# Another order of the loads and of ScalarE between the routing stage and the last stage of a PEER encoder layer

## The chip, the cores and the metric

The kernel runs on one NeuronCore of a Trainium2 chip. The metric is the device time of one launch in microseconds (us). Five engines take part, each with its own instruction stream in a fixed order: TensorE (PE in the views, its weight loads PEld), VectorE (DVE), ScalarE (ACT), GpSimd (POOL) and SyncE (SP), which here does nothing but issue DMAs. An engine that waits for a semaphore lets nothing of its own stream pass.

## What is computed

Two layers of attention, pooling and a PEER block (product-key retrieval over 128 x 128 experts). The attention part is left out here; the change lies in the PEER block:

```python
def peer_ffn(xn, wq, sub_keys, expert_u, expert_v):
    xc = xn.reshape((B * S) // PEER_CHUNK, PEER_CHUNK, D)
    def one(x):
        q = (x @ wq).reshape(C, PEER_HEADS, 2, PEER_HALF)
        s = jnp.einsum('chpk,hpnk->chpn', q, sub_keys)
        top_s, top_i = lax.top_k(s, K)
        ...                                    # the 16 best of 16 x 16 sums: experts e, weights g
        u = jnp.take(expert_u, e, axis=0)
        h = jax.nn.gelu(jnp.einsum('cd,chkd->chk', x, u))
        v = jnp.take(expert_v, e, axis=0)
        return jnp.einsum('chk,chkd->cd', g * h, v)
```

There are 512 tokens, D is 1024, and 16384 experts have one U row and one V row of 1024 each.

## The kernel before, in words

For three of the four token tiles (384 tokens) the kernel does not gather: it multiplies all tokens with all experts and weighs the result with a routing matrix that is zero for experts that were not chosen. The experts are cut into 128 **U blocks** and 128 **V blocks** of 128 experts (512 KB each). The fourth tile goes by gathered rows (128 slots of 1 MB, an indirect DMA from GpSimd each); VectorE does a dot product (`dot`, L1474) and an addition (`add_row`, L1480) for every slot, all through the stages below.

A U block goes through four steps. SP loads it into one of two buffers `RAW` (`load_experts`, L308; it waits until the block two before it has been split). ScalarE rounds it to its high part `RH` (`hi`, L855). VectorE or GpSimd takes the low part `RL` (`low`). TensorE multiplies both with the tokens (24 matmuls), and ScalarE applies gelu. Blocks 0 to 75 (FILLED is 76) are done ahead, their gelu is stored in DRAM (`gelu_dram`); blocks 76 to 127 are done in the last stage, four in a turn of 8 V blocks (`hidden` on TensorE, `hidden_gelu` on ScalarE, L1061).

In the **routing stage** TensorE makes the routing matrix beside the U blocks; ScalarE puts it into two staging buffers, and SP stores each batch of 48 tokens in four pieces (`store_routing`, L347). Batch 7 is the last; it lies in the second staging buffer.

In the **last stage**, 16 turns of 8 V blocks, a V block q goes like this. SP loads it into one of two buffers `VRAW` (`position`, L387; it waits until the V block two before it has been split). VectorE weighs gelu with routing, `WF` (L1542), from `GB` or `GEL` (gelu) and `GC` (routing read back from DRAM). ScalarE rounds V and WF to `VHI` (L1071) and `WHI` (L1073), VectorE takes the low parts `VLO` (L1546) and `WLO` (L1549). TensorE takes two V blocks at a time (`output`, 36 matmuls). After pairs 0 and 1 it does two U blocks of the next turn, after pairs 2 and 3 the other two.

What lies between the two stages is written out by hand on each engine. On SP, in this order: piece 0 of batch 7, U block 78 (`load_next(2)`), pieces 1 to 3, `GB` of turn 0, U block 79, then a wait until all routing stores have landed (`routing_kept`, L419), `GC` half 0, V blocks 0 and 1, the gelu store of block 74, `GC` half 1, U block 80, the gelu store of block 75, U block 81, a wait until all gelu stores have landed, and `positions(0, ...)`. That last function, with `begun=True`, issues U blocks 82 and 83 at q = 1 (L401, L402), each behind the split of the block two before it, and only then V block 2. On ScalarE: `hi` of 78 and 79, gelu of 76, `hi` of 80, gelu of 77, `hi` of 81, then V block 0. TensorE does 76 to 79 in a row, but 78 needs the gelu of 76 to be taken, and 79 that of 77 (L770). The low parts of 76 and 77 are VectorE's, those of 78 to 81 GpSimd's; GpSimd goes on to the gathers of slots 21 and up behind the low part of 81.

Of the kernel before, what the change touches and what calls it, by code (L numbers as in the profile page):

```python
# [58 lines left out]
FILLED = 76  # L59
FIRST = 34  # L60
# [57 lines left out]
def program(nc, x, pos, inv_freq, ident, edge, vecs, gains, stream, peer_keys, peer_u, peer_v, peer_rows, out):  # L118
# [3 lines left out]
    with ctx:  # L122
# [161 lines left out]
        def _(sp):  # L284
# [6 lines left out]
            with sp.Fori(0, LAYERS) as l:  # L291
# [21 lines left out]
                def store_gelu(f, slot):  # L313
                    sp.wait_ge(S.gelu_done, count(l, "gelu_done", f + 1))
                    sp.dma_start(gelus[f], GS[:, slot, :]).then_inc(sems[f"gelu_stored{slot}"], 16)
# [31 lines left out]
                def store_routing(b, piece):  # L347


                    keys = slice(NK // 4 * piece, NK // 4 * (piece + 1))  # L350
                    if piece == 0:
                        sp.wait_ge(S.routing_taken, count(l, "routing_taken", 12 * b + 12))
                    sp.dma_start(route[b, :, keys], STAGE[b % 2][:, keys, :]).then_inc(sems[f"routing_stored{b % 2}"], 16)
# [33 lines left out]
                def position(it, q):  # L387
                    sp.wait_ge(S.v_low, count(l, "v_low", 8 * it + q - 1))
                    sp.dma_start(VRAW[:, q % 2, :], peer_v[l, 8 * it + q]).then_inc(sems[f"v_loaded{q % 2}"], 16)
# [20 lines left out]
                def load_next(n):  # L410
                    load_experts(J_U + FILLED + n, FILLED + n, n % 2)
# [4 lines left out]
                        apart(sp)  # L416
                    sp.dma_start(GB[:], gelus.rearrange("(g i) p t -> p g i t", i=QUAD)[:, 0]).then_inc(S.gelu_loaded, 16)

                def routing_kept():  # L419
                    for s in range(2):  # L420
                        sp.wait_ge(sems[f"routing_stored{s}"], count(l, f"routing_stored{s}", 256))
                        apart(sp)

                def load_routing_of_first():
                    sp.dma_start(GC[:, 0].rearrange("p b i t -> p b (i t)"),
                                 route.rearrange("b p (g i) t -> p g b (i t)", i=QUAD)[:, 0]).then_inc(S.routing_loaded0, 16)

                store_routing(7, 0)
                load_next(2)
                for piece in range(1, 4):  # L430
                    store_routing(7, piece)
                load_gelus_of_first()
                load_next(3)
                routing_kept()
                load_routing_of_first()
                position(0, 0)
                position(0, 1)
                store_gelu(FILLED - 2, 2)
                load_new(0)
                load_next(4)  # L440
                store_gelu(FILLED - 1, 3)
                load_next(5)
                for s in range(4):
                    sp.wait_ge(sems[f"gelu_stored{s}"], count(l, f"gelu_stored{s}", 4 * FILLED))
                    apart(sp)
# [374 lines left out]
        def _(act):  # L820
# [32 lines left out]
            with act.Fori(0, LAYERS) as l:  # L853
# [221 lines left out]
                def positions(n, it, j, now, next1, next2):  # L1075
                    at_q, k = AT_Q[n], first_slot(n)
                    for q in range(8):
                        position(it, q)
                        if q - 1 in at_q:
                            score_next(k + at_q.index(q - 1) + 1, j)  # L1080
                        if q == 3:
                            for m in (2, 3):
                                if now:
                                    hidden_gelu(it, m)
                                if next1:
                                    hi(it + 1, J_U + FILLED + m)
                    if 7 in at_q:
                        score_next(k + at_q.index(7) + 1, j)
                    if next1:
                        for m in (0, 1):  # L1090
                            hidden_gelu(it + 1, m)
                            if next2:
                                hi(it + 2, J_U + FILLED + m)

                def score_next(k, j):
                    if k < SLOTS:
                        score(k + THREE * j, k % RING)

                hi(0, J_U + FILLED + 2)
                hi(0, J_U + FILLED + 3)  # L1100
                for m in (0, 1):
                    hidden_gelu(0, m)
                    hi(1, J_U + FILLED + m)
                positions(0, 0, 0, True, True, True)
                with act.Fori(0, 3) as j:
                    for n in (1, 2, 3):
# [27 lines left out]
        def _(dve):  # L1134
# [55 lines left out]
            with dve.Fori(0, LAYERS) as l:  # L1190
# [329 lines left out]
                for k in range(S_ROUTE, S_ROUTE + S_TURN):  # L1520
# [1 line left out]
                    add_row(k, k % RING)  # L1522
                    dot((k + 1) % RING, (k + 1) // RING)
                    dve.drain()
                for n in range(J_U + FIRST + R_FILLS + 1 + S_TURN, J_U + FILLED + 2):
                    low(0, n)
                dve.drain()

# [55 lines left out]
        @block.gpsimd  # L1584
        def _(pool):
            for name, value in STARTS.items():
                pool.sem_inc(sems[name], value)
            pool.iota(IOTA[:], [[1, P]], base=0, channel_multiplier=0,
                      allow_small_or_imprecise_dtypes=True).then_inc(iota_made, 1)
            with pool.Fori(0, LAYERS) as l:  # L1590
                def low(i, k):

                    pool.wait_ge(S.high_part, count(l, "high_part", 4 * i + k + 1))
                    pool.tensor_tensor(RL[:, k % 4, :], RAW[:, k % 2, :], RH[:, k % 4, :].bitcast(F32),  # L1594
                                       ALU.subtract).then_inc(S.low_part, 1)

                with pool.Fori(0, J_GATE // 4) as i:
                    for k in range(4):
                        low(i, k)
                low(0, J_GATE)  # L1600
                low(0, J_GATE + 1)


                pool.wait_ge(S.latent_summed, count(l, "latent_summed", 1))
                apart(pool)
                pool.memset(GAB[:, 0:KD, :], 1.0)
                pool.drain()
                with pool.Fori(0, 4) as i:
                    for k in range(4):
                        low(i, J_GATE + k + 2)  # L1610
                        n = 4 * i + k
                        pool.wait_ge(S.taken_by_act, count(l, "taken_by_act", 8 + n + 1))
                        gab = GAB[:, bass.ds(n, 1), :].rearrange("p o t -> p (o t)")
                        apart(pool)
                        pool.tensor_scalar(GATE[:, k % 2, :], GATE[:, k % 2, :], 0.5, 0.5, ALU.mult, ALU.add)
                        pool.drain()
                        pool.tensor_tensor(gab, gab, GATE[:, k % 2, :], ALU.mult).then_inc(S.gate_applied, 1)
                low(0, J_WO + 2)
                low(0, J_WO + 3)
                with pool.Fori(J_WO // 4 + 1, (J_U + FIRST - 2) // 4) as i:  # L1620
                    for k in range(4):
                        low(i, k)

                def gather(k):

                    pool.wait_ge(S.slot_done, count(l, "slot_done", k - 2))
                    apart(pool)
                    pool.indirect_dma_start(ROWS[:, k % RING, :], None, peer_rows,  # L1628
                                            bass.IndirectOffsetOnAxis(ap=LIST[:, k:k + 1], axis=0)).then_inc(
                                                sems[f"rows_gathered{k % RING}"], 16)  # L1630

                def low_of(n):
                    low(0, n)

                for n in range(4 * ((J_U + FIRST - 2) // 4), J_U + FIRST):
                    low_of(n)
                low_of(J_U + FIRST)
                pool.wait_ge(S.experts_listed, count(l, "experts_listed", 1))
                for k in range(RING):
                    gather(k)  # L1640
                for i in range(8):
                    for k in range(2):
                        gather(2 * i + k + RING)
                for k in range(S_TURN):
                    gather(S_ROUTE + k + RING)
                pool.wait_ge(S.low_part, count(l, "low_part", J_U + FILLED + 2))
                apart(pool)
                for n in range(J_U + FILLED + 2, J_U + FILLED + 6):
                    low_of(n)
                for it in range(16):  # L1650
                    for q in range(8):
                        if q in AT_Q[it]:
                            k = first_slot(it) + AT_Q[it].index(q) + RING
                            if k < SLOTS:
                                gather(k)
                        if q == 3 and it + 1 < FULL:
                            low_of(J_U + FILLED + 4 * it + 6)
                            low_of(J_U + FILLED + 4 * it + 7)
                    if it + 2 < FULL:
                        low_of(J_U + FILLED + 4 * it + 8)  # L1660
                        low_of(J_U + FILLED + 4 * it + 9)
# [73 lines left out]
```

## Time and profile before

| | us |
|---|---|
| median of 3 runs | 3322.99 (3320.5 to 3329.58) |
| profiled execution, its own time | 3319.98 |
| its span in the profile | 3318.2 |
| PE busy | 3167.9 (95%) |
| DVE busy | 2493.8 (75%) |
| ACT busy | 1334.9 (40%) |
| POOL busy | 1101.8 (33%) |

All sums are made on the profiled execution. Times in the rows count from the start of its span, so layer 0's passage from routing to last stage lies at 865 to 950 us, layer 1's at 2520 to 2605 us. A row of a timeline begins with the start and the duration; in brackets is the idle time of the engine just before it and what ended it. A busy PE is not PE at its peak: ends of matmuls are modelled.

### The profile page before, as it was taken

What the parts mean: (1) busy time and instruction counts of PE and PEld (TensorE: products, weight loads), DVE (VectorE), ACT (ScalarE), POOL (GpSimd) and SP (SyncE); (2) the same over time, 40 slices, a digit from 0 to 9 for tenths busy, and PEclk for the clock granted to TensorE, in tenths of its full rate; (3) what the DMA queues carried; (4) which work ended last, traced back from release to release, by engine and by line L of the source; (5) the groups of instructions that cost most, each with busy time, mean ns of one, the idle gap of its engine ahead of it and who ended that gap; (6) DMA issues with size and microseconds to landing.
All of it is one profiled execution on the core that took longest, in us unless ns stands there. A gap on an engine that the chain in (4) does not pass through costs nothing.

```text
span 3318.2 us, 52436 instructions
## 1 busy us (share of the span) xinstructions
PE 3167.9 (95%) x16946; PEld 2787.0 (84%) x16946; DVE 2493.8 (75%) x4216; ACT 1334.9 (40%) x2351; POOL 1101.8 (33%) x625
## 2 busy tenths in 40 slices
PE   7999999999799999999999999999998999999999
PEld 5887799899788888887878877998997888888877
DVE  4555499899588888887645544998995888988876
ACT  4343333355344334343444333333553343443434
POOL 3443354300134333341044433453001333334310
PEclk9999999999999999999999999999998999999999
DMA  3211244589899998988622112445898889999895
GB/s 110 83 51 51 102 132 132 184 303 326 316 348 328 335 331 325 336 323 328 222 96 70 51 57 102 133 134 183 312 324 321 330 319 344 343 336 348 328 333 200
DMA packets 249512, 774.05 MB, mean 233 GB/s; under 512 B 20352, under 2 KB 124928, under 8 KB 216320
## 3 DMA queue, kind: packets, MB, share of 16 engines
q1 hardware_dynamic: 212480, 503.53, 43.2%
q0 software_dynamic: 36864, 268.45, 21.4%
q8 instruction: 84, 1.38, 0.2%
q14 instruction: 84, 0.69, 0.1%
HBM read 689.59 MB, written 82.31 MB: 233 GB/s over the span
## 4 chain that ended last, share of the span: by engine, by line
PE 53%; DVE 13%; issue 11%; DMA 10%; DVEq 7%; ACT 4%; POOL 1%; SPq 0%; ACTq 0%; POOLq 0%
PE PS L468 16%; PE PS L470 15%; PE PS L469 15%; DMA VRAW<-in_peer_v 7%; DVEq L1560 6%; DVE ROWS L1474 4%; DVE VLO L1546 4%; PE PS L754 3%; DVE X L1480 2%; ACT VHI L1071 2%; PE PS L648 2%; DMA ROWS<-in_peer_rows,LIST 2%; DVE WLO L1549 1%; PE PS L710 1%; PE PS L642 1%
## 5 line engine op out<-in xcount | busy, mean ns | idle before, releaser
L468 PE MATMUL PS<-XH,RH 128*128 128x384 f32 (+1 forms) x2720 | 980.7, 361 | 38.4 <-ACT GEL L1063 25.7
L1594 POOL TENSOR_TENSOR RL<-RAW,RH 128x1024 fp32r<-128x1024 f32 x298 | 742.6, 2501 | 749.9 <-ACT RH L861 749.4
L469 PE MATMUL PS<-XL,RH 128*128 128x384 f32 (+1 forms) x2720 | 954.4, 351 | 0.0
L470 PE MATMUL PS<-XH,RL 128*128 128x384 f32 (+1 forms) x2720 | 954.4, 351 | 0.0
L1628 POOL DMA_INDIRECT ROWS<-in_peer_rows,LIST x256 | 291.1, 1137 | 1301.5 <-DVE X L1480 1260.4
L468 PE MATMUL PS<-VHI,WHI 128*128 128x512 f32 x1536 | 606.2, 395 | 45.9 <-DVE WLO L1549 45.8
L469 PE MATMUL PS<-VLO,WHI 128*128 128x512 f32 x1536 | 602.8, 392 | 0.0
L470 PE MATMUL PS<-VHI,WLO 128*128 128x512 f32 x1536 | 602.7, 392 | 0.0
L468 PEld LDWEIGHTS PS<-XH,RH 128*128 128x128 f32 x2720 | 515.1, 189 | 67.6 <-issue 27.0
L469 PEld LDWEIGHTS PS<-XL,RH 128*128 128x128 f32 x2720 | 515.6, 190 | 27.0
L470 PEld LDWEIGHTS PS<-XH,RL 128*128 128x128 f32 x2720 | 513.7, 189 | 28.7
L1546 DVE TENSOR_TENSOR VLO<-VRAW,VHI 128x1024 fp32r<-128x1024 f32 x256 | 317.0, 1238 | 198.5 <-ACT VHI L1071 198.3
L861 ACT ACTIVATE RH<-RAW 128x1024 fp32r<-128x1024 f32 x384 | 404.1, 1053 | 105.8 <-DMA RAW<-in_peer_u 46.8
L468 PEld LDWEIGHTS PS<-VHI,WHI 128*128 128x128 f32 x1536 | 291.5, 190 | 116.5 <-DVE VLO L1546 47.1
L1071 ACT ACTIVATE VHI<-VRAW 128x1024 fp32r<-128x1024 f32 x256 | 270.5, 1057 | 290.7 <-DMA VRAW<-in_peer_v 207.3
L470 PEld LDWEIGHTS PS<-VHI,WLO 128*128 128x128 f32 x1536 | 291.0, 189 | 61.4
L469 PEld LDWEIGHTS PS<-VLO,WHI 128*128 128x128 f32 x1536 | 291.6, 190 | 58.3
L1073 ACT ACTIVATE WHI<-WF 128x384 fp32r<-128x384 f32 x256 | 133.5, 522 | 511.7 <-DVE WF L1542 511.6
L1480 DVE SCALAR_TENSOR_TENSOR X<-ROWS,SHARE,X 128x1024 f32<-128x1024 f32 x256 | 326.8, 1277 | 7.4 <-ACT SHARE L1031 7.4
L1474 DVE SCALAR_TENSOR_TENSOR ROWS<-ROWS,XG 128x1024 f32<-128x1024 f32 x256 | 311.5, 1217 | 9.4 <-DMA ROWS<-in_peer_rows,LIST 9.4
L1542 DVE TENSOR_TENSOR WF<-GEL,GC 128x384 f32<-128x384 f32 x128 | 194.3, 1518 | 37.9 <-issue 37.9
L1549 DVE TENSOR_TENSOR WLO<-WF,WHI 128x384 fp32r<-128x384 f32 x256 | 189.1, 739 | 0.0
(235 smaller groups left out, 3318.5 us busy)
## 6 DMA issues: line engine op xcount, KB each, us to landing
RAW<-in_peer_u SPq DMA_DIRECT2D x256, 512.0 KB, 4.5
VRAW<-in_peer_v SPq DMA_DIRECT2D x256, 512.0 KB, 5.7
RAW<-in_stream SPq DMA_DIRECT2D x128, 512.0 KB, 3.5
route_dram<-STAGE SPq DMA_DIRECT2D x64, 768.0 KB, 6.9
GC<-route_dram SPq DMA_DIRECT2D x64, 768.0 KB, 10.4
gelu_dram<-GS SPq DMA_DIRECT2D x152, 192.0 KB, 4.6
GB<-gelu_dram SPq DMA_DIRECT2D x32, 768.0 KB, 12.6
GEL<-gelu_dram SPq DMA_DIRECT2D x6, 768.0 KB, 7.5
```

What stands on the lines that cost most here:

```text
L468: pe.matmul(acc, sh, mh, start=first, stop=False)
L469: pe.matmul(acc, sh, ml, start=False, stop=False)
L470: return pe.matmul(acc, sl, mh, start=False, stop=last)
L861: act.activation(RH[:, j % 4, :], RAW[:, j % 2, :], ACT.Copy).then_inc(S.high_part, 1)
L1071: act.activation(VHI[:, q % 4, :], VRAW[:, q % 2, :], ACT.Copy).then_inc(S.v_high, 1)
L1474: dve.scalar_tensor_tensor(ROWS[:, c, 0:D], ROWS[:, c, 0:D], 1.0, XG[:], ALU.mult, ALU.mult, accum_out=DOT[:, c:c + 1]).then_inc(S.dotted, 1)
L1480: dve.scalar_tensor_tensor(X[:, DT, :], ROWS[:, c, D:], SHARE[:, c:c + 1], X[:, DT, :], ALU.mult, ALU.add).then_inc(S.slot_done, 1)
L1546: dve.tensor_tensor(VLO[:, q % 4, :], VRAW[:, q % 2, :], VHI[:, q % 4, :].bitcast(F32), ALU.subtract).then_inc(S.v_low, 1)
L1549: dve.tensor_tensor(WLO[:, q % 4, :], WF[:, q % 2, :], WHI[:, q % 4, :].bitcast(F32), ALU.subtract).then_inc(S.weighted_low, 1)
L1560: dve.drain()
L1594: pool.tensor_tensor(RL[:, k % 4, :], RAW[:, k % 2, :], RH[:, k % 4, :].bitcast(F32), ALU.subtract).then_inc(S.low_part, 1)
L1628: pool.indirect_dma_start(ROWS[:, k % RING, :], None, peer_rows, bass.IndirectOffsetOnAxis(ap=LIST[:, k:k + 1], axis=0)).then_inc(sems[f"r ...
```

## The change

On SP, U block 79 is issued between pieces 1 and 2 of batch 7; `routing_kept` takes the buffers that it waits for, and only the first staging buffer is waited for ahead of V blocks 0 and 1 and U block 80. The wait for the second one, `GC` half 0 and half 1 and U block 81 stand behind them. On ScalarE, `hi` of 78 and gelu of 76, `hi` of 79 and gelu of 77 alternate, V blocks 0 and 1 come next, and `hi` of 80 and 81 stand behind V block 1. The low parts of 78 and 79 go from GpSimd to VectorE.

```diff
-                def routing_kept():
-                    for s in range(2):
+                def routing_kept(slots):
+                    for s in slots:
                         sp.wait_ge(sems[f"routing_stored{s}"], count(l, f"routing_stored{s}", 256))
                         apart(sp)
...
                 store_routing(7, 0)
                 load_next(2)
-                for piece in range(1, 4):
-                    store_routing(7, piece)
+                store_routing(7, 1)
+                load_next(3)
+                store_routing(7, 2)
+                store_routing(7, 3)
                 load_gelus_of_first()
-                load_next(3)
-                routing_kept()
-                load_routing_of_first()
+                routing_kept((0,))
                 position(0, 0)
                 position(0, 1)
+                load_next(4)
                 store_gelu(FILLED - 2, 2)
+                routing_kept((1,))
+                load_routing_of_first()
                 load_new(0)
-                load_next(4)
+                load_next(5)
                 store_gelu(FILLED - 1, 3)
-                load_next(5)
...
                         position(it, q)
                         if q - 1 in at_q:
                             score_next(k + at_q.index(q - 1) + 1, j)
+                        if q == 1 and n == 0:
+                            for m in (0, 1):
+                                hi(1, J_U + FILLED + m)
...
-                hi(0, J_U + FILLED + 2)
-                hi(0, J_U + FILLED + 3)
                 for m in (0, 1):
+                    hi(0, J_U + FILLED + 2 + m)
                     hidden_gelu(0, m)
-                    hi(1, J_U + FILLED + m)
...
-                for n in range(J_U + FIRST + R_FILLS + 1 + S_TURN, J_U + FILLED + 2):
+                for n in range(J_U + FIRST + R_FILLS + 1 + S_TURN, J_U + FILLED + 4):
                     low(0, n)
...
-                pool.wait_ge(S.low_part, count(l, "low_part", J_U + FILLED + 2))
+                pool.wait_ge(S.low_part, count(l, "low_part", J_U + FILLED + 4))
                 apart(pool)
-                for n in range(J_U + FILLED + 2, J_U + FILLED + 6):
+                for n in range(J_U + FILLED + 4, J_U + FILLED + 6):
                     low_of(n)
```

SP behind U block 79 of the kernel before; GC is the routing read back, VRAW a V block, RAW a U block, gelu_dram a gelu store:

```order
L421 ISA
L425 DMA GC<-route_dram 128x8x192 [waits routing_stored0,routing_stored1]
L388 REGISTER_ALU
L389 DMA VRAW<-in_peer_v 128x1024 [waits v_low]
L388 REGISTER_ALU
L389 DMA VRAW<-in_peer_v 128x1024 [waits v_low]
L314 REGISTER_ALU
L315 DMA gelu_dram<-GS 128x384 [waits gelu_done]
L375 REGISTER_ALU
L376 DMA GC<-route_dram 128x8x192 [waits weighted]
```

SP at the same place of the changed kernel, from the load of GB on:

```order
L421 ISA
L388 REGISTER_ALU [waits routing_stored0]
L389 DMA VRAW<-in_peer_v 128x1024 [waits v_low]
L388 REGISTER_ALU
L389 DMA VRAW<-in_peer_v 128x1024 [waits v_low]
L310 REGISTER_ALU
L294 ISA [waits low_part]
L294 DMA RAW<-in_peer_u 128x1024
L314 REGISTER_ALU
L315 DMA gelu_dram<-GS 128x384 [waits gelu_done]
L425 DMA GC<-route_dram 128x8x192 [waits routing_stored1]
```

The first GC load, which led this row of issues, now stands behind two V blocks, U block 80 and a gelu store, and the wait for the second staging buffer has moved with it.

ScalarE of the kernel before, from `hi` of 78 to the first V block (RH is a U block's high part, GEL a gelu, VHI and WHI the high parts of V and WF):

```order
L861 ACTIVATE RH<-RAW 128x1024 [waits block_used,block_loaded0]
L861 ACTIVATE RH<-RAW 128x1024 [waits block_used,block_loaded1]
L1062 REGISTER_ALU
L1063 ACTIVATE GEL<-PS 128x384 [waits block_used]
L858 REGISTER_ALU
L861 ACTIVATE RH<-RAW 128x1024 [waits block_used,block_loaded0]
L1062 REGISTER_ALU
L1063 ACTIVATE GEL<-PS 128x384 [waits block_used]
L861 ACTIVATE RH<-RAW 128x1024 [waits block_used,block_loaded1]
L1068 ISA
L1071 ACTIVATE VHI<-VRAW 128x1024 [waits pair_done,v_loaded0]
L1073 ACTIVATE WHI<-WF 128x384 [waits weighted]
```

ScalarE of the changed kernel, from the first V block to `hi` of 80 and 81 (lines have moved by two; ACTED and SHARE belong to a gathered slot):

```order
L1073 ACTIVATE VHI<-VRAW 128x1024 [waits pair_done,v_loaded0]
L1075 ACTIVATE WHI<-WF 128x384 [waits weighted]
L1073 ACTIVATE VHI<-VRAW 128x1024 [waits pair_done,v_loaded1]
L1075 ACTIVATE WHI<-WF 128x384 [waits weighted]
L1030 REGISTER_ALU
L1031 ACTIVATE ACTED<-DOT 128x1 [waits dotted]
L1033 ACTIVATE SHARE<-ACTED,GATES 128x1 [waits acted]
L860 REGISTER_ALU
L863 ACTIVATE RH<-RAW 128x1024 [waits block_used,block_loaded0]
L863 ACTIVATE RH<-RAW 128x1024 [waits block_used,block_loaded1]
```

The two high parts of 80 and 81 stood ahead of V block 0 and now stand behind WHI of V block 1.

## Rows read from the trace of the kernel before

**Rows 1.** Busy time by stretch: engines' busy us and count, granted clock, DMA share, GB/s
```profile
870.00:880.00 10.00, 10.00 (x60) 10.00 (x59) 3.66 (x4) 3.30 (x7) 2.76 (x2) 1.00 1.01 396
...
910.00:920.00 10.00, 7.44 (x27) 6.07 (x28) 9.52 (x15) 3.95 (x8) 2.97 (x3) 0.83 0.80 273
```

**Rows 2.** Timeline of PE, layer 0, from U block 78 to the fourth output pair
```profile
890.17 0.68 PE L468 MATMUL PS<-XH,RH 128*128 128x384 f32 x1 [8.29 <-ACT GEL L1063]
...
902.01 0.68 PE L468 MATMUL PS<-XH,RH 128*128 128x384 f32 x1 [5.21 <-ACT GEL L1063]
...
912.56 0.79 PE L468 MATMUL PS<-VHI,WHI 128*128 128x512 f32 x1 [4.67 <-DVE WLO L1549]
...
915.59 0.40 PE L469 MATMUL PS<-VLO,WHI 128*128 128x512 f32 x1
915.82 0.39 PE L470 MATMUL PS<-VHI,WLO 128*128 128x512 f32 x1
...
947.41 0.49 PE L468 MATMUL PS<-VHI,WHI 128*128 128x512 f32 x1 [0.42 <-DVE WLO L1549]
```

**Rows 3.** Waits of PE in layer 1 from 2520 us on: total, times, longest
```profile
PE PS L468 <- ACT GEL L1063: 12.2, 2, 8.8
```

**Rows 4.** Timeline of ACT, layer 0
```profile
888.61 1.06 ACT L861 ACTIVATE RH<-RAW 128x1024 fp32r<-128x1024 f32 x1 [10.31 <-DMA RAW<-in_peer_u]
...
902.16 1.06 ACT L861 ACTIVATE RH<-RAW 128x1024 fp32r<-128x1024 f32 x1 [0.28 <-DMA RAW<-in_peer_u]
903.13 1.04 ACT L1071 ACTIVATE VHI<-VRAW 128x1024 fp32r<-128x1024 f32 x1
...
910.93 0.52 ACT L1073 ACTIVATE WHI<-WF 128x384 fp32r<-128x384 f32 x1 [5.41 <-DVE WF L1542]
...
911.58 0.29 ACT L1031 ACTIVATE SHARE<-ACTED,GATES 128x1 f32<-128x1 f32 x1
912.21 1.06 ACT L1071 ACTIVATE VHI<-VRAW 128x1024 fp32r<-128x1024 f32 x1 [0.33 <-DMA VRAW<-in_peer_v]
```

**Rows 5.** Timeline of SP (issues of DMAs), layer 0
```profile
874.38 0.36 SPq L294 DMA_DIRECT2D RAW<-in_peer_u  x1
885.37 0.38 SPq L425 DMA_DIRECT2D GC<-route_dram  x1
885.97 1.25 SPq L389 DMA_DIRECT2D VRAW<-in_peer_v  x2
...
893.46 13.33 SPq L294 DMA_DIRECT2D RAW<-in_peer_u  x3
907.40 0.33 SPq L389 DMA_DIRECT2D VRAW<-in_peer_v  x1
```

**Rows 6.** Timeline of DVE, layer 0
```profile
892.66 0.56 DVE L1542 TENSOR_TENSOR WF<-GB,GC 128x384 f32<-128x384 f32 x1 [18.46 <-DMA GC<-route_dram]
...
910.34 0.56 DVE L1542 TENSOR_TENSOR WF<-GB,GC 128x384 f32<-128x384 f32 x1 [0.16 <-issue]
...
915.00 0.56 DVE L1542 TENSOR_TENSOR WF<-GB,GC 128x384 f32<-128x384 f32 x1 [0.16 <-issue]
915.48 1.22 DVE L1546 TENSOR_TENSOR VLO<-VRAW,VHI 128x1024 fp32r<-128x1024 f32 x1
...
921.28 0.55 DVE L1549 TENSOR_TENSOR WLO<-WF,WHI 128x384 fp32r<-128x384 f32 x1
...
924.41 5.75 DVE L1542 TENSOR_TENSOR WF<-GEL,GC 128x384 f32<-128x384 f32 x1 [0.24 <-issue]
```

**Rows 7.** Timeline of POOL, layer 0: pairs of low parts
```profile
901.58 4.71 POOL L1594 TENSOR_TENSOR RL<-RAW,RH 128x1024 fp32r<-128x1024 f32 x2 [9.49 <-ACT RH L861]
...
951.59 5.75 POOL L1594 TENSOR_TENSOR RL<-RAW,RH 128x1024 fp32r<-128x1024 f32 x2 [1.16 <-ACT RH L861]
```

**Rows 8.** DMA issue of V block 0 (885.97): KB, us from issue to landing
```profile
VRAW<-in_peer_v SPq DMA_DIRECT2D x1, 512.0 KB, 7.9
```

**Rows 9.** DMA issue of V block 2 (907.40), the same columns
```profile
VRAW<-in_peer_v SPq DMA_DIRECT2D x1, 512.0 KB, 4.8
```

## The prediction

> **What bounds the kernel now.** I read the page's busy line first (TensorE is 95% busy, so a gain must come from its gaps), then TensorE's timeline for its gaps at the place of the change, then the timelines of the engine that ends each gap, and last the landings of the DMAs behind them.
>
> In layer 0 TensorE stops three times between U block 77 and the first output pair: 8.29 us ahead of block 78, 5.21 ahead of 79, 4.67 ahead of the pair [rows 2]. In layer 1 the first two are 12.2 us together [rows 3]. The first two wait for ScalarE's gelu, and the reader is to see why that is late: it stands behind `hi` of block 79, whose load was issued at 874.38 [rows 5] and reached ScalarE at 888.61, after 14.2 us [rows 4]. The DMA engines are full there (share 1.01 at 870 to 880 [rows 1]). The third gap waits for VectorE, and that wait is the one that counts: the last stage cannot start before V blocks 0 and 1 and their WF are split. VectorE made WF of block 0 at 892.66, as soon as the routing had landed, but WF of block 1 only at 910.34 [rows 6], since ScalarE's in-order stream stood at `hi` of 80 and 81 until 903.13 [rows 4]. From there VectorE paces: 4.66 us for each V block (910.34 to 915.00), and WLO of block 3 ends at 921.83 (921.28 and 0.55) [rows 6]. TensorE's first pair runs from 912.56 to about 922.2: 7 matmuls take 3.03 us, the other 29 take 0.23 each, 6.6 [rows 2]. So at pair 1 VectorE and TensorE arrive within half a us of each other, and at pair 3 TensorE waits 0.42 [rows 2]. I measure the change at WLO of block 3 and at pair 3.
>
> **TensorE's own gaps: worth nothing by themselves.** U block 79 cannot be issued earlier: its load waits for the split of 77, which let it go at 874.38 before, and does now. It lands earlier only because two routing pieces and GB no longer stand ahead of it. Then blocks 78 and 79 follow 77 without a gap, and TensorE is done with them long before VectorE has the first pair ready. It then waits for WLO of block 1. The cover of this edit is that wait; if 79 landed late as before, nothing would change either. VectorE splits 78 and 79 in a stretch in which it stood still for 18.46 us [rows 6], so that move is free too.
>
> **The first half, a gain.** V blocks 0 and 1 no longer stand behind 80 and 81 on ScalarE, so WF of block 0 decides, and that waits for the first GC load. GC could not be issued before the last routing store landed (issued at 885.37 [rows 5]), and it now stands in SP's queue behind V blocks 0 and 1, U block 80 and a gelu store. V block 0, issued right behind GC, landed at 885.97 + 7.9 = 893.9 [rows 5, 8], 1.3 us after GC: that is what 512 KB costs in the full queue. The routing stores themselves end 1.3 us later (79 ahead of two of them); that is no added cost, as GC stood behind 79 before as well. Three blocks at 1.3 and 192 KB at 0.5 make 4.4 us: WF of block 0 at 892.66 + 4.4 = 897.1. Bounds: 0, if the queue delays GC not at all, and 5.7, if the later routing stores count in full. One V block takes 4.66, so WF of block 1 starts at 901.8 and ends at 902.3, against 910.9: **8.6 us earlier**.
>
> **The second half, the gain given back.** V block 2 stands on SP behind U blocks 82 and 83, whose loads wait for the splits of 80 and 81. Before, these were made while V block 0 was still waiting: GpSimd's pair of them ran at 901.58 for 4.71 [rows 7], SP got past at 906.79 (893.46 and 13.33), and V block 2 went out at 907.40 [rows 5]. Now `hi` of 80 and 81 come after WHI of block 1, so the chain runs from the end of WF of block 1 (call it 0):
> - WHI of 1 and the slot's SHARE: 910.93 to 911.87 in [rows 4], so 0.9 to 1.0.
> - `hi` of 80: 1.06 [rows 4], done at 2.0. `hi` of 81 follows beside GpSimd.
> - GpSimd's two low parts: 4.71 with VectorE out of the way, 5.75 with VectorE at work [rows 7]. VectorE is at work on slots here, so I take 5.75: 7.8.
> - SP issues 83, then V block 2: 906.29 to 906.79 before for the one, as much again for the other, so 1.0: 8.8.
> - V block 2 lands: 4.8 [rows 9]. It has the same two U blocks ahead of it as before, so I take this, 13.6; the row of the full queue, 7.9 [rows 8], is the other end.
> - VHI 1.06 [rows 4], VLO of 2 at 14.7. From there to the end of WLO of 3 it was 915.48 to 921.83, 6.35 [rows 6]: 21.05.
>
> Before, the same way took 921.83 - 910.90 = 10.93. The loss is **10.1 us**. Net at WLO of block 3: 10.1 - 8.6 = +1.5.
>
> **TensorE's clock.** Pair 0 now starts 8.6 earlier, at about 904, and takes 9.6 as before, and TensorE then stands still for over 9 us until WLO of block 3 at 923.4. After the stop of 4.67 us its first 7 matmuls went at 0.43 us instead of 0.23, and the granted clock of 910 to 920 was 0.83 [rows 1, 2], a mean of the two levels 1.2 and 2.4 GHz. I charge the same again for pair 1: 7 x 0.2 = 1.4. Pair 1 starts 1.2 later than before (923.4 against 922.2); with 1.4 more and 0.42 of slack at pair 3 [rows 2] that is 2.2 for TensorE, 1.5 for VectorE. I take 2 in each layer.
>
> **Sum.** The profiled execution took 3319.98 us (span 3318.2, and 1.8 around it). Two layers at +2 give 3324. The median of the three runs is 3.0 above that execution, so the forecast on its scale is **3327**. About 0.3% (10 us) is what a measurement of this kernel tells from no change; this is inside.
>
> **A rule of the Trainium skill against the change.** GpSimd's pair took 4.71 us in one place and 5.75 in the other, and a WF that takes 0.56 elsewhere took 5.75 at 924.41 [rows 6, 7]: the two engines hinder each other. The Trainium skill, SBUF — State Buffer, "Who interferes with whom", says that a VectorE operation with two SBUF inputs and a GpSimd operation take an exclusive pair of ports, each for its whole instruction, whichever starts first. By it both slot instructions could go ahead of a low part; as an estimate with VLO's 1.22 for each, the pair ends 4.71 + 2.4 long, 1.4 later than I took, and the forecast would be 3330. The trace shows one such turn (5.75 is 1.04 over 4.71), not two.
>
> **Rival 1, GC is not delayed** (DMAs overlap, and the small reads of GC slip between the blocks). WF of block 0 stays at 892.66, 4.4 earlier than taken, and GpSimd's pair takes 4.71: net at WLO of 3 is 1.5 - 4.4 - 1.0 = -3.9, with TensorE's cold start about -2.5 to -4 in a layer. 3315 to 3318 on the scale of the runs. For it: landings are pipelined. Against it: V block 0 landed after GC, in the order of issue [rows 8]. Chance 0.14.
>
> **Rival 2, the gain stays** because V block 2 is free as soon as VLO of block 0 is done, as before. Then the whole last stage starts 8.6 us earlier in both layers: 3306. It decides by whether SP reaches V block 2 before the split of 81; the code puts 82 and 83 ahead. Chance 0.06.
>
> **Rival 3, slower: V block 2 lands late.** The gathers of slots 21 and 22 stand on GpSimd behind the low part of 81, and with VectorE early their slots are free, so both go out in one go exactly when V blocks 2 and 3 do, behind 82 and 83. If V block 2 takes the 7.9 us of a full queue [rows 8] instead of 4.8, that is 3.1 more; a second turn of VectorE ahead of GpSimd adds about 1.2, and a layer costs 2 + 3.1 + 1.2 = 6.3, the kernel +13: 3336. It becomes slower by over 0.3% from about 3 us more than my sum in a layer, that is a landing of 7.8. For it: a busy queue costs that much 20 us earlier. Against it: the queue has run dry by then. Chance 0.18.
>
> The Trainium skill, DMA: Bandwidth & Descriptors, "Queues, rings and completion order", adds that a DMA engine goes round the queues packet by packet, so SP's V blocks and GpSimd's gathers would share; an estimate by it doubles V block 2's 1.3, +1.3 in a layer, which no row here shows apart.
>
> **How the numbers follow.** Forecast as summed 0.62, rivals 0.14, 0.06, 0.18. Forecast and rival 1 are within 0.3%: 0.76; faster 0.06; slower 0.18. The forecast's own bounds are about 3323 to 3331; with rival 1 below and the near part of rival 3 above the range is 3315 to 3335.
>
> **What would show it.** In the changed trace: TensorE without the waits for GEL (right for the first edit), WF of block 0 at 896 to 898, GpSimd's pair of low parts behind WHI of block 1, V block 2 issued 8 to 9 us after WF of block 1, a new stop of TensorE of 8 to 10 us between pair 0 and pair 1, and `WLO` of block 3 at 922 to 925. It is wrong if WF of block 0 stays below 894, if V block 2 is issued before the low part of 81, or if V block 2's landing takes over 8 us.

## The result, and the profile after

The change makes the kernel slightly slower: **3332.02 us**, the median of 12 runs (3321.41 to 3338.95), against 3316.74 for 12 runs of the kernel before beside it (3305.94 to 3329.58). The ratio is **1.0042, with a 95% interval of 1.0029 to 1.0056**. The profiled execution took 3326.28 us, with a span of 3324.5. The forecast was 3327 and the range 3315 to 3335, so the time lies inside; but the loss of 0.42% is over the 0.3% that I had named as what a measurement can tell, and I had given a loss of that size only 18%.

In the passage from routing to the last stage nearly everything went as summed. TensorE's timeline in layer 0, from U block 78 to the second output pair (start, duration, in brackets the idle time ahead and what ended it), answers to [rows 2]:

```profile
901.61 0.79 PE L470 MATMUL PS<-VHI,WHI 128*128 128x512 f32 x1 [12.52 <-DVE WLO L1552]
...
920.90 0.79 PE L470 MATMUL PS<-VHI,WHI 128*128 128x512 f32 x1 [8.18 <-DVE WLO L1552]
921.49 0.63 PE L471 MATMUL PS<-VLO,WHI 128*128 128x512 f32 x1
921.91 0.63 PE L472 MATMUL PS<-VHI,WLO 128*128 128x512 f32 x1
```

The three stops have become two. No wait for GEL is left, in neither layer; both stops wait for VectorE's WLO. The timeline of VectorE (DVE) over the same stretch answers to [rows 6]:

```profile
894.74 0.56 DVE L1545 TENSOR_TENSOR WF<-GB,GC 128x384 f32<-128x384 f32 x1 [10.21 <-DMA GC<-route_dram]
...
899.39 0.56 DVE L1545 TENSOR_TENSOR WF<-GB,GC 128x384 f32<-128x384 f32 x1 [0.16 <-issue]
...
902.67 3.39 DVE L1477 SCALAR_TENSOR_TENSOR ROWS<-ROWS,XG 128x1024 f32<-128x1024 f32 x1
906.00 0.08 DVE L1477 DVE_READ_ACCUMULATOR ROWS<-ROWS,XG 128x1 f32 x1
906.23 2.49 DVE L1545 TENSOR_TENSOR WF<-GB,GC 128x384 f32<-128x384 f32 x1 [0.16 <-issue]
914.42 1.23 DVE L1549 TENSOR_TENSOR VLO<-VRAW,VHI 128x1024 fp32r<-128x1024 f32 x1 [5.69 <-ACT VHI L1073]
...
920.22 0.55 DVE L1552 TENSOR_TENSOR WLO<-WF,WHI 128x384 fp32r<-128x384 f32 x1
```

WF of V blocks 0 and 1 now come 4.65 us apart (before 17.68 [rows 6]), and the time gained is lost again behind WF of block 2: VLO of block 2 waits 5.69 us for VHI. The reason stands on SP (issues of DMAs) and on GpSimd (POOL), which answer to [rows 5, 7]; the last row is V block 2's landing (KB, us from issue to landing), as in [rows 9]:

```profile
873.24 0.35 SPq L294 DMA_DIRECT2D RAW<-in_peer_u  x1
...
885.94 0.40 SPq L425 DMA_DIRECT2D GC<-route_dram  x1
...
905.15 3.66 SPq L294 DMA_DIRECT2D RAW<-in_peer_u  x2
909.00 11.80 SPq L389 DMA_DIRECT2D VRAW<-in_peer_v  x4
```

```profile
901.96 6.34 POOL L1597 TENSOR_TENSOR RL<-RAW,RH 128x1024 fp32r<-128x1024 f32 x2 [29.48 <-ACT RH L863]
```

```profile
VRAW<-in_peer_v SPq DMA_DIRECT2D x1, 512.0 KB, 4.3
```

GpSimd begins the low parts of 80 and 81 only at 901.96, SP gets past U blocks 82 and 83 behind them, and V block 2 goes out at 909.00.

**Where the loss is.** I compared the starts of WLO, one for each V block, between the two traces. Between the last WLO of turn 0 and the last WLO of turn 11 the kernel before takes 564.35 us in layer 0 and 558.05 in layer 1, the changed one 571.49 and 564.86: 7.1 and 6.8 more, in a stretch in which the change alters no instruction. One trace of each kernel cannot price the loss: in the seven traces of the experiments below this stretch of a layer takes 550.5 to 571.3 us, and the kernel before lies among them. But the two traces show what is new. VectorE's waits in layer 0, 960 to 1560 us (total, times, longest), in the kernel before:

```profile
DVE VLO L1546 <- ACT VHI L1071: 59.9, 22, 3.7
DVE WF L1542 <- issue: 27.3, 96, 0.8
```

and in the changed kernel:

```profile
DVE VLO L1549 <- ACT VHI L1073: 53.6, 18, 5.8
DVE WF L1545 <- issue: 45.8, 94, 7.8
```

"issue" is idle time in which the engine waits for nothing that the profile shows. It was 0.8 us at most ahead of a WF, and is now 7.8, with 18.5 us more in all. The long ones stand at the start of turns 4, 7 and 10 in both layers. VectorE's timeline at turn 4 of layer 0, before:

```profile
1101.17 0.08 DVE L1474 DVE_READ_ACCUMULATOR ROWS<-ROWS,XG 128x1 f32 x1
1102.05 0.56 DVE L1542 TENSOR_TENSOR WF<-GB,GC 128x384 f32<-128x384 f32 x1 [0.79 <-issue]
1105.55 1.27 DVE L1546 TENSOR_TENSOR VLO<-VRAW,VHI 128x1024 fp32r<-128x1024 f32 x1 [2.95 <-ACT VHI L1071]
1106.74 2.75 DVE L1549 TENSOR_TENSOR WLO<-WF,WHI 128x384 fp32r<-128x384 f32 x1
...
1111.99 0.56 DVE L1542 TENSOR_TENSOR WF<-GB,GC 128x384 f32<-128x384 f32 x1 [0.16 <-issue]
```

and after:

```profile
1105.88 0.08 DVE L1477 DVE_READ_ACCUMULATOR ROWS<-ROWS,XG 128x1 f32 x1
1112.95 0.56 DVE L1545 TENSOR_TENSOR WF<-GB,GC 128x384 f32<-128x384 f32 x1 [6.99 <-issue]
1113.42 1.22 DVE L1549 TENSOR_TENSOR VLO<-VRAW,VHI 128x1024 fp32r<-128x1024 f32 x1
1114.56 0.55 DVE L1552 TENSOR_TENSOR WLO<-WF,WHI 128x384 fp32r<-128x384 f32 x1
...
1117.61 0.56 DVE L1545 TENSOR_TENSOR WF<-GB,GC 128x384 f32<-128x384 f32 x1 [0.16 <-issue]
```

Turns 1 to 12 are a hardware loop on VectorE (`dve.Fori(0, 4)`, three turns to a pass), so turns 4, 7 and 10 are the places where it returns to its start. A stop of 7 us costs much less than 7: from the last row of the old turn to WF of the second block it is 10.74 us before (1101.25 to 1111.99) and 11.65 after (1105.96 to 1117.61), since before VectorE waited there for VHI, 2.95, and its WLO took 2.75 instead of 0.55. The lateness of the WLO starts against the kernel before grows, from the last V block ahead of a return to the second one behind it, by 0.96, 1.81, 1.53, 1.64, 0.82 and 0.79 us at the six returns, 7.6 together. That is 7.6 of the 13.9 us above; the rest lies between the returns, where the two executions drift apart and together by some us. The page's lists of DMA queues (packets, MB, share) say where to look: the kernel before has

```profile
q14 instruction: 84, 0.69, 0.1%
```

and the changed one

```profile
q14 instruction: 115, 0.93, 0.1%
```

These are 31 packets of instructions more. At each of the six returns the trace has four of them, 8 KB each, inside the stop or just behind it (at 1110, 1110, 1115 and 1119 us for turn 4); most of the others come once in each pass.

What the change has to do with that loop is a count. It moves the low parts of U blocks 78 and 79 from GpSimd to VectorE, two instructions each (a register operation and the subtraction) in VectorE's program *ahead* of the loop. The loop stands 4 instructions later than before.

### The profile page after: what moved, and what is told of

The parts are those of the page before. It is cut to its first block, busy times and chain, and to the rows that moved or that the text cites. A ratio compares the mean times of both kernels' runs of the same rounds, so it can differ in the third digit from the quotient of the medians.

```text
span 3324.5 us, 52436 instructions
## 1 busy us (share of the span) xinstructions
PE 3158.4 (95%) x16946; PEld 2775.1 (83%) x16946; DVE 2490.4 (75%) x4220; ACT 1336.3 (40%) x2351; POOL 1088.8 (33%) x621
## 4 chain that ended last, share of the span: by engine, by line
PE 53%; DVE 13%; issue 12%; DMA 10%; DVEq 7%; ACT 3%; POOL 1%; ACTq 0%; SPq 0%; POOLq 0%
PE PS L470 16%; PE PS L472 15%; PE PS L471 15%; DMA VRAW<-in_peer_v 7%; DVEq L1563 6%; DVE VLO L1549 4%; DVE ROWS L1477 4%; PE PS L756 3%; DVE X L1483 2%; PE PS L650 2%; ACT VHI L1073 1%; DVE WLO L1552 1%; DMA ROWS<-in_peer_rows,LIST 1%; POOL RL L1597 1%; PE PS L712 1%
## 5 line engine op out<-in xcount | busy, mean ns | idle before, releaser
L1597 POOL TENSOR_TENSOR RL<-RAW,RH 128x1024 fp32r<-128x1024 f32 x294 | 730.4, 2494 | 758.4 <-ACT RH L863 757.9
L992 ACT ACTIVATE GS<-PS 128x384 f32<-128x384 f32 x152 | 74.8, 492 | 273.8 <-PE PS L472 273.6
```

## The experiments

Theory A, formed from this: the stops come from where the loop stands in the program. The rivals were that the stops belong to what the change does in the passage (VectorE splitting 78 and 79, its order against GpSimd), and that the passage itself costs the whole loss, with the stops harmless.

**e1: the kernel before, with nothing changed but the loop's place.** Four memsets of one column each, on VectorE, ahead of the `dve.drain()` that stands before the last stage:

```
+                for i in range(4):
+                    dve.memset(HGB[:, i:i + 1], 0.0)
                 dve.drain()
```

> The kernel before, with four extra one-element writes on VectorE (64 ns kind, into a tile that is dead there) between the last low part and V block 0, where VectorE stands still for 18 us. Nothing else moves; every later VectorE instruction lies four further in its program, as in the changed kernel. Theory A (the loss comes from the place of VectorE's loop over the turns in its program: at each return the loop has to be loaded again): the stops of about 7 us at the start of turns 4, 7 and 10 appear here too, and the kernel gets 8 to 15 us slower than before, ratio 1.0025 to 1.0045. Theory B (the loss comes from the passage: TensorE's new stop and cold start, and the phase in which the last stage begins): no change, ratio 0.999 to 1.001.

Measured: ratio 1.0023 (1.0008 to 1.0038). The waits of VectorE, 960 to 1560 us:

```profile
DVE WF L1544 <- issue: 47.8, 96, 8.1
```

There are stops of 6.8 to 8.1 us at turns 4, 7 and 10 of both layers, and 114 instruction packets. Nothing else of the change is in this kernel, so the stops come from the place, and they cost it about 0.23%, 7.6 us: 1.3 us for each return, as in the steps above. The ratio is just under the 1.0025 that theory A had as its lower end.

**e2: the change, with the two low parts back on GpSimd**, so that the loop stands where it stood before:

```
-                for n in range(J_U + FIRST + R_FILLS + 1 + S_TURN, J_U + FILLED + 4):
+                for n in range(J_U + FIRST + R_FILLS + 1 + S_TURN, J_U + FILLED + 2):
...
-                pool.wait_ge(S.low_part, count(l, "low_part", J_U + FILLED + 4))
+                pool.wait_ge(S.low_part, count(l, "low_part", J_U + FILLED + 2))
...
-                for n in range(J_U + FILLED + 4, J_U + FILLED + 6):
+                for n in range(J_U + FILLED + 2, J_U + FILLED + 6):
```

> The changed kernel with one part undone: the low parts of U blocks 78 and 79 stay on GpSimd, so VectorE's program is that of before, instruction for instruction, while SP and ScalarE have the new order. Theory A: the stops at turns 4, 7 and 10 are gone, and the time is that of before within 4 us, ratio 0.999 to 1.001. Theory B: as slow as the changed kernel, ratio about 1.004.

Measured: ratio 1.0001 (0.9983 to 1.0019). VectorE's waits in the same stretch:

```profile
DVE WF L1545 <- issue: 27.4, 97, 0.8
```

Without the four instructions no return stops, with the rest of the change in place. VectorE's wait ahead of WF of block 0 is 21.7 us (10.2 in the changed kernel, 18.46 before), and no loss of time can be measured.

**e3 and e5: the change, with the loop moved further on.** VectorE keeps the low parts; 124 memsets (e3) or 16 (e5) put the loop 128 or 20 instructions later than in the kernel before. They run while VectorE waits for GC.

```
+                for i in range(124):
+                    dve.memset(NUMBER[:, i:i + 1], 0.0)
                 dve.drain()
```

> The changed kernel with 124 extra one-element writes on VectorE at the same place (about 7 us in a stretch where it waits for 10), so that its loop over the turns lies 128 instructions behind its place in the kernel before. Theory A, if programs are loaded in pieces of 128 instructions (the 8 KB of the instruction queue's packets at 64 bytes each): the stops are gone again, ratio 0.999 to 1.002. If the pieces are larger: stops remain, ratio about 1.004. Theory B: ratio about 1.004.

> The change plus 16 memsets of one column on VectorE, so that its loop over the last stage stands 20 instructions later than in the kernel before (the change alone: 4 later, with stops of 6 to 7 us at the loop's return; 128 later: none). Theory A, three blocks: instructions come in blocks and the engine holds two; the loop of 271 instructions spans three blocks only if it begins within about 15 instructions of a place that recurs every 256. The kernel before does not stop and 4 later does, so 20 later is past the narrow zone: no stops ahead of WF (wait for issue back to 0.8 us on average), instruction packets back to about 84, ratio 1.0000 to 1.002 to the kernel before. Theory B, a broad zone (any place from 4 later up to some 100): stops of 7 us as in the change, ratio 1.003 to 1.005. Theory C, the stops have nothing to do with the loss: no stops, yet a ratio of 1.004.

Measured: e3 1.0020 (1.0005 to 1.0036), e5 1.0020 (1.0000 to 1.0040). The waits of VectorE in e3, then in e5, and e5's instruction packets:

```profile
DVE WF L1547 <- issue: 28.0, 99, 0.8
```

```profile
DVE WF L1547 <- issue: 26.7, 98, 0.8
```

```profile
q14 instruction: 84, 0.69, 0.1%
```

The stops are gone in both, so the place that stops is narrow: 4 instructions on it stops, 20 on and 128 on it does not. That is theory A as e5's text puts it, and the broad zone falls. The size of the pieces stays open: e3's text had the stops gone only with pieces of 128 instructions, but a narrow zone that recurs every 256 fits these four places as well. Both ratios are under the changed kernel's 1.0042, though both kernels do *more* on VectorE. Theory C, no stops and yet 1.004, is at the very end of e5's interval; e1, where the stops alone cost time, speaks against it.

**e6: the changed kernel itself again**, on the chip and beside the kernels of e5 and e7.

> The changed kernel itself, on the same chip as the two beside it, so that its ratio to the kernel before can be set against theirs. Theory A: 1.003 to 1.005, stops at turns 4, 7 and 10 of both layers, and the kernel with 16 memsets more is 0.2 to 0.4% faster than this one though it does more. If the loss was the chip's of the first measurement: about 1.000 here.

Measured: 1.0054 (1.0033 to 1.0074), with 114 instruction packets and stops of 7.3 to 8.6 us at the six returns:

```profile
DVE WF L1545 <- issue: 46.9, 94, 8.6
```

The loss is not the first chip's. Against e5's 1.0020 the stops are worth 1.0054 / 1.0020 = 1.0034, somewhat more than e1's 1.0023. The intervals of all three are wide, so I put the stops at 0.2 to 0.35%.

The table gathers the closing branch of the loop, read from the branch instructions in VectorE's trace: the time from the branch to the next instruction, a register operation that waits for nothing.

| kernel | loop later by | three returns of layer 0, us | of layer 1, us | q14 packets | ratio |
|---|---|---|---|---|---|
| before | 0 | 0.32, 0.27, 0.27 | 0.28, 0.26, 0.26 | 84 | 1 |
| changed | 4 | 6.17, 7.00, 6.73 | 6.83, 6.02, 5.99 | 115 | 1.0042 |
| e1 | 4 | 7.04, 7.32, 6.64 | 6.60, 6.95, 6.01 | 114 | 1.0023 |
| e6 | 4 | 6.51, 7.78, 6.93 | 7.22, 6.89, 7.04 | 114 | 1.0054 |
| e2 | 0 | 0.32, 0.27, 0.27 | 0.28, 0.26, 0.26 | 84 | 1.0001 |
| e5 | 20 | 0.35, 0.32, 0.31 | 0.32, 0.29, 0.29 | 84 | 1.0020 |
| e3 | 128 | 0.33, 0.30, 0.29 | 0.33, 0.30, 0.29 | 86 | 1.0020 |

In the kernels whose return stops, the lateness of WLO grows there as in the changed one: by 0.8 to 2.1 us in e1, 9.4 together, and by 1.3 to 2.6 in e6, 11.2 together. In e2 to e5 and e7 it grows by 0.02 at most. Such a step spans a few us of each execution, so the drift between executions hardly touches it. TensorE's weight loads, ScalarE and GpSimd return to their loops in the last stage within 0.06 to 0.26 us in every kernel, so of these engines VectorE's loop alone stops.

One pass of the loop is 273 instruction records from one closing branch to the next. The same engine's outermost loop, over the two layers, is a jump back over the whole program: it stops in every kernel, 5.30 us in the one before and 3.96 to 5.51 in the others. So a jump back that stops takes VectorE some 4 to 8 us, and one that does not 0.3.

The Trainium skill, Runtime: NRT & Kernel Launch, "Instruction fetch mechanics", has the rule for this: an engine takes in its instructions in blocks of 16 KiB, 256 instructions, holds two of them, and a taken branch to a place outside the two has to wait for a load. The traces agree: by that rule, as an estimate, a loop of 273 lies in two blocks at most places and in three at about 16 of 256, which fits a stop at 4 and none at 0, 20 or 128. The page gives no price for such a wait; here it is 6.0 to 7.8 us. That the place decides is shown by the runs; that the blocks are the reason is the page's account, which no run here shows by itself.

**e4: V block 2 first.** The second half of my sum says that V block 2 is late because it stands behind U blocks 82 and 83 on SP. From e2, one line (q is the V block after whose issue SP goes on to the next U blocks, `begun` is turn 0):

```
-                        if q == 1:
+                        if q == (3 if begun else 1):
```

> As the second kernel (low parts of 78 and 79 on GpSimd, VectorE's program that of before), and on SP, in turn 0, V blocks 2 and 3 ahead of U blocks 82 and 83. It prices the wait that gives back the gain: V block 2 then goes out as soon as VLO of block 0 is done. If that wait is what eats the gain (my sum: 10 us in a layer), VectorE reaches WLO of block 3 some 8 us earlier than before, TensorE's second stop is about 0 to 1 us, and the kernel is 12 to 17 us faster than before, ratio 0.995 to 0.9965. If the gain is eaten elsewhere, ratio 0.999 to 1.001.

Measured: 0.9989 (0.9971 to 1.0007), far less than the 0.995 to 0.9965 of the main expectation: most of the gain is lost elsewhere. WLO of block 3 starts 45.75 us after the low part of U block 77 in layer 0 and 48.11 in layer 1, against 48.49 and 49.30 in e2. V block 2 is no longer late; the timeline of VectorE shows what is late next:

```profile
903.50 2.49 DVE L1545 TENSOR_TENSOR WF<-GB,GC 128x384 f32<-128x384 f32 x1 [0.16 <-issue]
...
912.58 1.23 DVE L1477 SCALAR_TENSOR_TENSOR ROWS<-ROWS,XG 128x1024 f32<-128x1024 f32 x1 [3.78 <-DMA ROWS<-in_peer_rows,LIST]
```

A gathered row (ROWS) holds VectorE's dot product for 3.78 us, and with it WF of block 3. GpSimd had issued its gather only behind the two low parts (e4's GpSimd):

```profile
899.21 6.37 POOL L1597 TENSOR_TENSOR RL<-RAW,RH 128x1024 fp32r<-128x1024 f32 x2 [16.71 <-ACT RH L863]
905.73 1.09 POOL L1631 DMA_INDIRECT ROWS<-in_peer_rows,LIST  x1 [0.15 <-issue]
```

**e7: the row first as well.** e4, with GpSimd's first gather of the last stage ahead of the low parts of 80 and 81:

```
-                for n in range(J_U + FILLED + 2, J_U + FILLED + 6):
+                for n in range(J_U + FILLED + 2, J_U + FILLED + 4):
                     low_of(n)
...
                                 gather(k)
+                        if it == 0 and q == 0:
+                            for n in range(J_U + FILLED + 4, J_U + FILLED + 6):
+                                low_of(n)
```

> The change with the low parts of U blocks 78 and 79 back on GpSimd, with V blocks 2 and 3 loaded ahead of U blocks 82 and 83 in turn 0, and now also with GpSimd's gather of the first row of the last stage ahead of its split of U blocks 80 and 81. In the version without this last step the dot product ahead of WF of V block 3 waited 3.8 us for that row, which stood 6.4 us behind the split. Theory: V block 3 comes 3 to 4 us earlier in each layer, and the whole ends at 0.996 to 0.998 of the kernel before. Rival: the next wait (the V blocks of turn 0's second half, or the split that now ends 1 us later) takes it back, and the ratio stays at 0.998 to 1.000, as without the step (0.9989).

Measured: 0.9997 (0.9980 to 1.0015), as the rival said. In its trace the step does what it should: WLO of block 3 comes 43.22 and 43.03 us after the low part of 77, where the kernel before has 48.31 and 47.37, and TensorE's second stop is down to

```profile
915.54 0.49 PE L470 MATMUL PS<-VHI,WHI 128*128 128x512 f32 x1 [2.40 <-DVE WLO L1552]
```

That is 4.3 to 5.1 us a layer, 9.4 or 0.28% in all, and the interval ends at 0.20%. So by this one trace a part of it is lost again further on. The second pair of turn 1 on TensorE still starts 5.1 us earlier after the low part of 77 than in the kernel before, in both layers, so it is lost later than that; where was not followed to the end of the stage. A next wait is to be seen in the trace, 1.78 us for the next gathered row at 918.39. Neither e4 nor e7 can be told from the kernel before.

## Why the prediction was right, and where it was wrong

**TensorE's gaps are worth nothing by themselves: right.** The waits for GEL are gone in both layers, the time is not: TensorE waits 12.52 and 8.18 us for WLO instead.

**The first half: right, with the delay of GC somewhat too large.** Counted from the issue of U block 79 (874.38 before [rows 5], 873.24 after), WF of block 0 moved from +18.28 to +21.50, 3.2 us later; I had taken 4.4. The end of WF of block 1 moved from +36.52 to +26.71, 9.8 earlier against 8.6. Rival 1, no delay of GC at all, falls. WF of block 0 itself is at 894.74 and WLO of block 3 at 920.22, each a little ahead of the signs that I had given (896 to 898, 922 to 925), mostly since U block 79 was issued 1.1 us earlier in this execution.

**The second half: right nearly to the step.** From the end of WF of block 1 (899.95) V block 2 goes out after 9.05 us (said 8.8), it lands in 4.3 (said 4.8), VLO of block 2 starts at 14.47 (said 14.7) and WLO of block 3 ends at 20.82 (said 21.05). Errors inside it cancel: GpSimd's pair of low parts took 6.34, not 5.75, while SP then had V block 2 out after 0.7 us instead of 1.0 and the landing took 4.3 instead of 4.8. Beside the pair VectorE's dot product took 3.39, where the next takes 1.22 at 917.22, and WF of block 2 took 2.49 instead of 0.56; that cost nothing here, as VectorE then waited 5.69 for VHI. The estimate that the prediction worked out from the Trainium skill, SBUF — State Buffer, "Who interferes with whom", 7.1 for the pair, was further off to the other side. The net at WLO of block 3 was +0.1 in layer 0 (+1.5 forecast) and, from the low part of 77, +1.5 in layer 1. The eight layers of the four kernels that share this passage (changed, e3, e5, e6) have 49.18 us on average from the low part of 77 to WLO of block 3, the four of the two with the old passage (before, e1) 47.20: +2.0, where the sum had +1.5. The spread is wide, 47.93 to 52.91 against 45.64 to 48.31. TensorE's pair 3, counted the same way, starts 1.8 us later on average, where I took 2.

Rival 2, the gain stays, falls. Rival 3 gave 3336, closest to the result in size, but its mechanism did not occur: V block 2 landed in 4.3 us, not 7.9.

**TensorE's clock: right in kind.** After each stop the granted clock is a mean of the two levels, 1.2 and 2.4 GHz: 0.64 for 900 to 910 and 0.78 for 920 to 930. The first matmuls of pair 1 start 0.42 us apart (921.49 and 921.91 above), much as before after a stop of 4.67 us (0.43); eight go at that pace, where I had charged seven. The rows of the changed kernel (busy time by stretch, as [rows 1]; clock, DMA share and GB/s are the last three):

```profile
900.00:910.00 10.00, 8.39 (x25) 6.68 (x26) 8.56 (x6) 2.80 (x5) 7.59 (x4) 0.64 0.19 65
...
920.00:930.00 10.00, 9.10 (x33) 7.40 (x34) 9.76 (x7) 4.57 (x10) 5.89 (x3) 0.78 0.96 323
```

The DMA share of 0.19 shows the price of the order on SP: with V block 2 behind 82 and 83, the DMA engines are nearly empty in the ten us at whose end it goes out.

**The step that failed** is the sentence "VectorE splits 78 and 79 in a stretch in which it stood still for 18.46 us, so that move is free too." The time on VectorE was free: its wait for GC shrank from 18.46 to 10.21. The place was not. Two low parts are four instructions more ahead of a loop of 273, and 220 us later its return stops for 6 to 7 us, three times in each layer. By the ratios this term is 0.23 to 0.34%, 8 to 11 us, where I had nothing, and no rival of mine had it. Without it, e3 and e5 give 1.0020 with intervals of 1.0005 to 1.0036 and 1.0000 to 1.0040; my sum of +4 us is 1.0012 and lies in both. So these runs do not contradict the sum for what it counted, and the verdict "no measurable change" was wrong because of a term that was left out.

**That the time lies in the range is luck.** The forecast stood on three runs of the kernel before, with a median of 3322.99; twelve have 3316.74. Against that median the sum of +4 is 3321 and the range ends at 3329, under the measured 3332. The high base, and a range that reached up to rival 3, made room for a loss whose larger part neither the sum nor a rival contained.

What stays open: whether the 0.2% of e3 and e5 is the passage alone (+4 us are 0.12%). e2, with the low parts on GpSimd, has 1.0001 (0.9983 to 1.0019), which neither confirms nor excludes a further cost; in its trace TensorE's pair 3 starts as late as in the others. No run moves the two low parts alone, without the new order on SP and ScalarE.

## What to carry to other kernels

Ask of every moved instruction not only when it runs but what stands behind it in its engine's program: a handful of instructions anywhere ahead of a hardware loop can push it to a place where its return stops. A long "issue" wait of one instruction, at regular places, with more packets on an instruction queue, is the sign; a few more dummy instructions ahead of the loop, 16 here, are the cheap test, and here they took the stops away. And a gain at the head of a queue is worth only what the next thing in that queue lets through: V blocks 0 and 1 came 9.8 us earlier, and first V block 2, then a gathered row, took it back.

## What was not expected of the hardware

- The return of a loop costs 0.26 to 0.35 us at one place of the program and 5.99 to 7.78 at another, 4 instructions on. The zone is narrow: 20 on it is 0.29 to 0.35 again.
- The jump back over the layer loop stops VectorE for 3.96 to 5.51 us in every kernel, the one before among them.
- The changed kernel's six stops, 39 us together, cost 8 to 11 us of the whole; at the one return that is shown above, VectorE had waited 2.95 for VHI in the kernel before.
- While GpSimd made its two low parts (6.34 us against 4.71 [rows 7]), VectorE's dot product took 3.39 us and its WF 2.49, instead of 1.22 and 0.56: both engines took longer.
